# An SBUF allocator that rounds every buffer to 128 bytes in place of 64, in a two-layer mixer plus sparse-attention kernel on one core

## The chip, the cores and the metric

The kernel runs on one NeuronCore of one Trainium2 chip. The metric is the device time of one launch, in microseconds (us). All times below are of the hardware: either of plain runs, or of one execution that the hardware profiler recorded.

## The reference

The input is `x`, 512 tokens of 1024 channels, all in fp32. Two layers of a hybrid block come first, then one layer of sparse attention (NSA):

```python
for l in range(2):                       # first_block
    h = rmsnorm(x, norm_mix_g[l])
    proj = h @ w_in[l]                   # 1024 -> mLSTM q, k, v, o and gates, attention q, k, v, two branch gates
    hm = mlstm(...)                      # 4 heads, chunkwise
    ha = sliding_window_attention(...)   # 16 query heads, 4 key heads, window 128
    y = sigmoid(ga) * (hm @ w_branch_m[l]) + sigmoid(gb) * (ha @ w_branch_a[l])
    x = x + y @ w_out[l]
    h = rmsnorm(x, norm_mlp_g[l])
    x = x + square(relu(h @ w_up[l])) @ w_down[l]      # 1024 -> 4096 -> 1024
x = rmsnorm(x, final_norm_g)
u = rmsnorm(x, pre_norm_gain_2[0])       # second_block, one layer
out = x + rmsnorm(nsa_mixer(u, ...), post_norm_gain_2[0])
```

## The kernel before

Every activation is kept transposed: channels on the 128 partitions, the 512 tokens along the free axis, so that a 1024 x 512 activation is eight tiles `[128, 512]` of 2048 bytes per partition.

**Units.** Every weight matrix is cut into units of 1024 inputs by 128 outputs. One unit makes one `[128, 512]` output tile in PSUM. The 332 units of 512 KB come from `w_all` through one queue (SyncE, L426) into `w_raw`, two buffers in turn. Products are made in three parts so that fp32 precision is nearly kept with the faster fp32r type: ScalarE writes `w_hi` (the weights rounded to fp32r, L861), GpSimd writes `w_lo` (the rest, L446), and each activation likewise has a `hi` and a `lo` buffer. For each of the eight input tiles `quarter()` issues three matmuls of 512 columns: `w_hi` by `hi` (L485), `w_hi` by `lo` (L486) and `w_lo` by `hi` (L487). A unit is thus 24 matmuls, in four quarters of six. The stationary operand of each is a 128 x 128 block of `w_hi` or `w_lo` (512 bytes per partition), which TensorE loads (LDWEIGHTS, shown as PEld) while the matmul before still streams its 2048 bytes.

**Which buffer streams in which product.** The steps of the prediction need this list:

| buffers that stream | product | units of 24 matmuls in the whole kernel |
|---|---|---|
| `hT_hi/lo` | everything in the attention loops (`LOOP`, `NLOOP`), NSA's keys and values, the MLP's `up` | 200 |
| `hm_hi/lo` (the same bytes as `hT`) | `hm @ w_branch_m` (`MIX`) | 16 |
| `ha_hi/lo` | `ha @ w_branch_a` (`MIX`) | 16 |
| `y_hi/lo` | `y @ w_out`, two layers and NSA | 24 |
| `u_hi/lo` | the MLP's `down` | 64 |
| `hx_hi/lo` | the first products of each layer, before the norm is known | 12 |

`MIX` takes units of `hm` and `ha` in turn. The MLP runs four times per layer eight units of `up` and then eight of `down`. Two gate products of 24 matmuls (`gate_gemm`, L512 to L514) stream `hx` against weights of their own, `gw_hi/lo`, and a third streams `hT` against `gwn_hi/lo`. In the attention loops the quarters of the `hT` units are placed among short matmuls and transposes (the transposes have `ident` as the moving operand).

**The order of work** is written out by hand as lists of steps (`LOOP`, `MIX`, `MLP`, `NLOOP`, ...), and each engine walks the same lists; semaphores tie them together. Nothing in them depends on addresses.

**The allocator.** `new()` gives every buffer its byte offset within the partition. Without `at=` it takes the next free place, counted in `top`; with `at=a` it takes the next place of a list `a`, so that the same region can be laid out several times for different stages. The size is rounded up to 64 bytes before it is added. The first buffer starts at byte 16512, which is 129 times 128. The large buffers have sizes that are multiples of 512, so the offset of one buffer carries on to all behind it. The small ones do not: `vn` (96 bytes), `vcur` (80), `late` (4), then `vbuf` and `numsb` (4128 each), `gcur` (32).

Of the kernel before, what the change touches and what calls it, by code (L numbers as in the profile page):

```python
# [222 lines left out]
def two_layers_and_nsa(nc, w_all, wg_all, vec_it, vec_l, vec_n, ident_in, tri_in, onehot_w, onehot_n,  # L223
                       tab_w, tab_n, late_in, x_in, w1_in, w2_in, pos_in, scr_w, scr_n, out):
    ctx = ExitStack()
    with ctx:
# [5 lines left out]
        top = [base]  # L232

        def new(name, shape, dt=F32, at=None):
            size = -(-4 * int(np.prod(shape[1:])) // 64) * 64
            off = top[0] if at is None else at[0]
            t = nc.alloc_sbuf_tensor_at(name, shape, dt, offset=off)
            if at is None:
                top[0] += size
            else:  # L240
                at[0] += size
            return t

        x = new("x", [P, KT, S])
        hT_at = top[0]
        hT = [new("hT_hi", [P, KT, S], F32R), new("hT_lo", [P, KT, S], F32R)]
        raw = new("w_raw", [P, 2, KT * P])
        w_hi = new("w_hi", [P, 4, HALF], F32R)
        w_lo = new("w_lo", [P, 4, HALF], F32R)
# [1673 lines left out]
```

How the kernel before makes its waits and increments, by code:

```python
        @block.sync  # L410
        def _(sp):
            nc.sync.dma_start(vl[:, 0:DEPTH, :], vec_l).then_inc(gains_in, 16)
            nc.sync.dma_start(x[:, 0, :], x_in[0:P, :]).then_inc(x_landed[0], 16)
            nc.sync.dma_start(raw[:, 0, :], w_all[0]).then_inc(raw_in[0], 16)
            for k in range(2, KT, 2):
                nc.sync.dma_start(x[:, k, :], x_in[k * P:(k + 1) * P, :]).then_inc(x_landed[k], 16)
            nc.sync.dma_start(raw[:, 1, :], w_all[1]).then_inc(raw_in[1], 16)
            for dst, src in ((ident[:, :], ident_in), (tri[:, :], tri_in), (vit[:, :, :], vec_it),
                             (vn[:, :], vec_n), (late[:, :], late_in)):
                nc.sync.dma_start(dst, src).then_inc(cst_in, 16)
            with sp.Fori(0, UNITS // 2 - 1) as i:
                for p in range(2):
                    sp.wait_ge(lo_done, i * 4 + 2 * p + 6)
                    nc.sync.dma_start(raw[:, p, :], w_all[2 * i + p + 2]).then_inc(raw_in[p], 16)
            for k in range(KT):
                if k % 2 == 0:
                    sp.wait_ge(x_done, KT + k // 2 + 1)
                else:
                    sp.wait_ge(x_pool, k // 2 + 1)
                nc.sync.dma_start(out[k * P:(k + 1) * P, :], x[:, k, :]).then_inc(out_s, 16)
            sp.wait_ge(out_s, 16 * KT)
# [56 lines left out]
            def norm_sum(count, total=None):  # L491
                use = step_uses(w, ("norm_",))[0]
                pe.wait_ge(o_free[1], use.m + 1)
                pe.wait_ge(sq_used, count)
```

## Time and profile before

| | |
|---|---|
| median of 3 runs | 2405.76 us |
| lowest and highest | 2405.76 and 2406.56 us |
| the profiled execution's own time | 2405.57 us |
| its span, first to last instruction | 2403.5 us |
| mean granted TensorE clock | 0.982 |
| busy: TensorE matmul, weight load | 96%, 80% |
| busy: VectorE, ScalarE, GpSimd | 38%, 40%, 37% |
| DMA | 193.84 MB, 81 GB/s on average |

The chain of waits is the work that ended last, followed back from the end. In the timeline each row is one instruction; on TensorE the ends of matmuls are modelled, so that two neighbouring rows overlap in time, and what one matmul costs in a dense stretch is the distance between two starts.

### The profile page before, as it was taken

To read this page: it belongs to the slowest core of one execution; us is meant where nothing else is said; L and a number is where in the kernel's file an instruction comes from. 1 tells how busy PE (TensorE), PEld (TensorE's weight loads), DVE (VectorE), ACT (ScalarE), POOL (GpSimd) and SP (SyncE) were. 2 spreads that over 40 slices of the span, in tenths; PEclk is the share of its full clock that TensorE was granted. 3 is DMA by queue.
4 is the path that set the end of the run, shared out by engine and by line. 5 is a ranking of instruction groups with operands and counts; after the bars stand their busy time and mean duration, and the time that the engine had idled before them with its cause. 6 is when DMAs were issued, how large, how long until landed. Compare 5 with 4: busy or idle time off the path is not lost.

```text
span 2403.5 us, 35769 instructions
## 1 busy us (share of the span) xinstructions
PE 2317.2 (96%) x11397; PEld 1917.0 (80%) x11397; DVE 920.9 (38%) x1907; ACT 972.0 (40%) x2051; POOL 885.2 (37%) x672
## 2 busy tenths in 40 slices
PE   6999999999999998999999999999999999999996
PEld 4888888788888886888888788888887878888885
DVE  7343343324132136243343324132136335445452
ACT  4455455434232234455455434222234244445443
POOL 3333333444444444333333444444444321221213
PEclk9999999999999999999999999999999999999998
DMA  3221222222222222221222222222223221110202
GB/s 121 70 77 63 87 70 70 79 87 96 97 97 96 96 91 93 70 79 61 87 71 69 79 89 94 97 97 96 96 89 117 104 71 53 44 64 32 70 35 70
DMA packets 58793, 193.84 MB, mean 81 GB/s; under 512 B 6654, under 2 KB 11311, under 8 KB 58352
## 3 DMA queue, kind: packets, MB, share of 16 engines
q1 hardware_dynamic: 50400, 177.48, 21.7%
q10 hardware_dynamic: 8336, 15.60, 1.9%
q8 instruction: 36, 0.59, 0.1%
q14 instruction: 21, 0.17, 0.0%
HBM read 190.89 MB, written 2.16 MB: 80 GB/s over the span
## 4 chain that ended last, share of the span: by engine, by line
PE 89%; DVE 5%; ACT 2%; issue 2%; ACTq 0%; DVEq 0%; POOL 0%; POOLq 0%
PE ps L485 25%; PE ps L487 24%; PE ps L486 24%; PE ps L547 4%; PE ps L527 3%; PE ps L535 2%; PE ps L645 1%; PE ps L501 1%; PE ps L633 1%; PE ps L786 1%; PE ps L748 1%; PE ps L811 1%; DVE sz L1363 0%; DVE tn L1805 0%; ACT e_buf L908 0%
## 5 line engine op out<-in xcount | busy, mean ns | idle before, releaser
L446 POOL TENSOR_TENSOR w_lo<-w_raw,w_hi 128x512 fp32r<-128x512 f32 x664 | 878.6, 1327 | 1497.4 <-ACT w_hi L861 1493.5
L485 PE MATMUL ps<-hT_hi,w_hi 128*128 128x512 f32 x1600 | 653.6, 409 | 0.6 <-DVE qn L1333 0.6
L487 PE MATMUL ps<-hT_hi,w_lo 128*128 128x512 f32 x1600 | 630.9, 394 | 0.0
L486 PE MATMUL ps<-hT_lo,w_hi 128*128 128x512 f32 x1600 | 630.2, 394 | 0.0
L861 ACT ACTIVATE w_hi<-w_raw 128x512 fp32r<-128x512 f32 x664 | 411.3, 626 | 483.3 <-PE ps L487 455.3
L487 PEld LDWEIGHTS ps<-hT_hi,w_lo 128*128 128x128 f32 x1600 | 304.0, 190 | 66.8
L485 PEld LDWEIGHTS ps<-hT_hi,w_hi 128*128 128x128 f32 x1600 | 305.0, 191 | 64.4 <-issue 8.6
L486 PEld LDWEIGHTS ps<-hT_lo,w_hi 128*128 128x128 f32 x1600 | 305.1, 191 | 56.3 <-issue 0.5
L485 PE MATMUL ps<-u_hi,w_hi 128*128 128x512 f32 x512 | 201.7, 394 | 0.0
L486 PE MATMUL ps<-u_lo,w_hi 128*128 128x512 f32 x512 | 201.7, 394 | 0.0
L487 PE MATMUL ps<-u_hi,w_lo 128*128 128x512 f32 x512 | 201.7, 394 | 0.0
L1397 DVE TENSOR_TENSOR x<-x,ps 128x512 f32<-128x512 f32 x64 | 44.1, 688 | 267.4 <-PE ps L487 267.4
L1370 DVE SCALAR_TENSOR_TENSOR e_buf<-ps,rs 128x512 f32<-128x512 f32 x64 | 44.3, 692 | 213.2 <-PE ps L487 213.2
L487 PEld LDWEIGHTS ps<-u_hi,w_lo 128*128 128x128 f32 x512 | 95.7, 187 | 23.8
L485 PEld LDWEIGHTS ps<-u_hi,w_hi 128*128 128x128 f32 x512 | 95.8, 187 | 23.7
L486 PEld LDWEIGHTS ps<-u_lo,w_hi 128*128 128x128 f32 x512 | 95.8, 187 | 23.6
L912 ACT ACTIVATE u_hi<-e_buf 128x512 fp32r<-128x512 f32 x64 | 40.6, 634 | 175.0 <-DVE e_buf L1370 175.0
L991 ACT ACTIVATE Pn<-Ln,st 128x128 f32<-128x128 f32 (+3 forms) x128 | 71.7, 560 | 91.1 <-DVE st L1471 89.8
L991 ACT ACTIVATE Pb<-L,st 128x256 f32<-128x256 f32 (+1 forms) x128 | 61.4, 480 | 73.7 <-DVE st L1471 72.6
L1471 DVE CUSTOM_DVE_ANT_0 Ln<-ps,biasn 128x128 f32<-128x128 f32 (+3 forms) x128 | 62.1, 490 | 51.2 <-DVEq L1278 48.8
L1333 DVE SCALAR_TENSOR_TENSOR aq<-ps,aq 64x512 fp32r<-64x512 f32 x32 | 22.0, 689 | 154.3 <-ACT aq L886 153.7
L485 PE MATMUL ps<-y_hi,w_hi 128*128 128x512 f32 x192 | 75.9, 395 | 1.9 <-DVE y_lo L1813 1.9
(289 smaller groups left out, 3326.0 us busy)
## 6 DMA issues: line engine op xcount, KB each, us to landing
w_raw<-w_all SPq DMA_DIRECT2D x332, 512.0 KB, 3.2
bias<-scr_w ACTq DMA_DIRECT2D x8, 512.0 KB, 3.8
biasn<-scr_n ACTq DMA_DIRECT2D x4, 1024.0 KB, 5.2
w1k<-w_in ACTq DMA_DIRECT2D x2, 1024.0 KB, 8.4
w1v<-w_in ACTq DMA_DIRECT2D x1, 2048.0 KB, 15.0
out<-x SPq DMA_DIRECT2D x8, 256.0 KB, 2.0
x<-x_in SPq DMA_DIRECT2D x4, 256.0 KB, 6.3
x<-x_in ACTq DMA_DIRECT2D x4, 256.0 KB, 5.7
```

The costliest lines, as they stand in the source:

```text
L446: nc.gpsimd.tensor_tensor(w_lo[:, h, :], raw[:, h // 2, (h % 2) * HALF:(h % 2 + 1) * HALF], w_hi[:, h, :].bitcast(F32), ALU.subtract).then ...
L485: nc.tensor.matmul(ps[:, p, :], wh, hi[:, kk, :], start=(kk == 0), stop=False)
L486: nc.tensor.matmul(ps[:, p, :], wh, lo[:, kk, :], start=False, stop=False)
L487: last = nc.tensor.matmul(ps[:, p, :], wl, hi[:, kk, :], start=False, stop=(kk == KT - 1))
L527: last = nc.tensor.matmul(ps[:, 2 + us[0].b, 0:nk * P], q[:, hd, qt * P:(qt + 1) * P], kk[i][:, k0 * P:(qt + 1) * P], start=(i == 0), stop ...
L535: last = nc.tensor.transpose(ps[:, 4 + us[0].b, c * P:(c + 1) * P], pb[:, j % 3, c * P:(c + 1) * P], ident[:, :])
L547: last = nc.tensor.matmul(ps[:, 6 + ob, (qt % 2) * 256 + hd * DH:(qt % 2) * 256 + (hd + 1) * DH], pt[:, j % 3, c * P:(c + 1) * P], vv[:, k ...
L861: nc.scalar.activation(w_hi[:, 2 * p + h, :], raw[:, p, h * HALF:(h + 1) * HALF], ACT.Copy)\
L991: nc.scalar.activation(Pbuf[:, j % 3, 0:n], Lbuf[:, j % 2, 0:n], ACT.Exp, scale=-1.0, bias=st[:, 0, j:j + 1], accum_out=st[:, 1, j:j + 1]) ...
L1370: V.scalar_tensor_tensor(e_buf[:, e.b, :], g, 0.0, rs[:, :], ALU.max, ALU.mult).then_inc(g_free[u.b], 1)
L1397: V.tensor_tensor(x[:, n, :], x[:, n, :], g, ALU.add).then_inc(g_free[u.b], 1)
L1471: V.tensor_tensor_reduce(out=Lbuf[:, j % 2, 0:n], in0=ps[:, 2 + b_, 0:n], in1=reverse(bias_t, j % GH, n), scale=1.0, scalar=first, op0=ALU ...
```

## The change

One number in `new()`:

```diff
         def new(name, shape, dt=F32, at=None):
-            size = -(-4 * int(np.prod(shape[1:])) // 64) * 64
+            size = -(-4 * int(np.prod(shape[1:])) // 128) * 128
             off = top[0] if at is None else at[0]
```

What it does to the offsets follows from the code alone. The buffers from `x` to `late` stay where they are. `late` holds 4 bytes and now takes 128 in place of 64, so everything behind it moves by 64 bytes. In the attention loop's layout `vbuf` and `numsb` add 64 bytes each, so what follows them moves by 192. The offset within 512 bytes, of the buffers that the prediction names:

```
buffer                      before: offset, mod 512     after: offset, mod 512
hT_hi (hm_hi)                32896   128                 32896   128
w_hi, w_lo                   73856   128  82048  128     the same
ident                        90240   128                 the same
u_hi (u_lo 16384 behind)     97856    64                 97920   128
gw_hi                       101952    64                102016   128
y_hi, hx_hi                 130624    64                130688   128
ha_hi                       163392    64                163456   128
mqk                         163392    64                163456   128
Pb (behind vbuf, numsb)     208576   192                208768   384
gwn_hi                      220736    64                220800   128
```

Both layouts end below the limit that the code asserts, 229368 (before 228928, after 228992), and no two buffers overlap after that did not before.

## Rows read from the trace of the kernel before

**Rows 1.** The page: span, TensorE's busy time, and the chain's shares by engine.

```profile
span 2403.5 us, 35769 instructions
...
PE 2317.2 (96%) x11397; PEld 1917.0 (80%) x11397; DVE 920.9 (38%) x1907; ACT 972.0 (40%) x2051; POOL 885.2 (37%) x672
...
PE 89%; DVE 5%; ACT 2%; issue 2%; ACTq 0%; DVEq 0%; POOL 0%; POOLq 0%
```

**Rows 2.** Busy us (count) by stretch: PE, PEld, DVE, ACT, POOL; granted clock; DMA.

```profile
575.00:607.00 32.00, 32.00 (x142) 26.47 (x141) 14.03 (x18) 11.64 (x20) 17.53 (x13) 1.00 0.26 91
615.00:657.00 42.00, 42.00 (x182) 33.66 (x181) 5.52 (x8) 9.93 (x16) 20.14 (x16) 1.00 0.29 95
```

**Rows 3.** Timeline, TensorE, mixing products: start us, us, engine, line, operation.

```profile
441.08 0.39 PE L485 MATMUL ps<-ha_hi,w_hi 128*128 128x512 f32 x1
...
446.68 0.39 PE L485 MATMUL ps<-hm_hi,w_hi 128*128 128x512 f32 x1
...
448.06 0.39 PE L485 MATMUL ps<-hm_hi,w_hi 128*128 128x512 f32 x1
...
452.14 0.39 PE L485 MATMUL ps<-ha_hi,w_hi 128*128 128x512 f32 x1
```

**Rows 4.** Timeline, TensorE, from the `w_out` product to the second `up`.

```profile
524.10 0.39 PE L485 MATMUL ps<-y_hi,w_hi 128*128 128x512 f32 x1
...
568.90 0.39 PE L485 MATMUL ps<-hT_hi,w_hi 128*128 128x512 f32 x1
...
613.35 0.39 PE L485 MATMUL ps<-u_hi,w_hi 128*128 128x512 f32 x1
...
658.15 0.39 PE L485 MATMUL ps<-hT_hi,w_hi 128*128 128x512 f32 x1
...
701.69 0.39 PE L485 MATMUL ps<-u_hi,w_hi 128*128 128x512 f32 x1
```

**Rows 5.** Timeline, TensorE, layer 0: the gate product, then a V unit.

```profile
33.15 0.39 PE L512 MATMUL ps<-hx_hi,gw_hi 128*128 128x512 f32 x1
...
35.19 0.40 PE L485 MATMUL ps<-hx_hi,w_hi 128*128 128x512 f32 x1
...
37.06 0.40 PE L487 MATMUL ps<-hx_hi,w_lo 128*128 128x512 f32 x1
```

**Rows 6.** Timeline, TensorE, the last layer's gate product.

```profile
1856.59 0.39 PE L512 MATMUL ps<-hT_hi,gwn_hi 128*128 128x512 f32 x1
...
1859.34 0.39 PE L512 MATMUL ps<-hT_hi,gwn_hi 128*128 128x512 f32 x1
```

**Rows 7.** Groups by form, TensorE: mean ns of one after the comma.

```profile
L486 PE MATMUL ps<-u_lo,w_hi 128*128 128x512 f32 x512 | 201.7, 394 | 0.0
...
L486 PE MATMUL ps<-y_lo,w_hi 128*128 128x512 f32 x192 | 75.7, 395 | 0.0
...
L486 PE MATMUL ps<-ha_lo,w_hi 128*128 128x512 f32 x128 | 50.4, 394 | 0.0
...
L486 PE MATMUL ps<-hx_lo,w_hi 128*128 128x512 f32 x96 | 39.5, 411 | 0.0
```

**Rows 8.** Timeline, TensorE: `hT` quarters among the mLSTM products.

```profile
113.02 0.40 PE L486 MATMUL ps<-hT_lo,w_hi 128*128 128x512 f32 x1
...
115.33 0.39 PE L487 MATMUL ps<-hT_hi,w_lo 128*128 128x512 f32 x1
```

**Rows 9.** Groups by form, TensorE: short matmuls.

```profile
L535 PE MATMUL ps<-ident,Pb 128*128 128x128 f32 x224 | 46.9, 279 | 5.0 <-DVE hm L1627 4.6
...
L633 PE MATMUL ps<-mqk 128*128 128x128 f32 x160 | 23.0, 274 | 0.0
```

**Rows 10.** Groups by form, VectorE.

```profile
L1397 DVE TENSOR_TENSOR x<-x,ps 128x512 f32<-128x512 f32 x64 | 44.1, 688 | 267.4 <-PE ps L487 267.4
...
L1387 DVE TENSOR_TENSOR y_lo<-t,y_hi 128x512 f32 x16 | 11.1, 693 | 14.1 <-ACT y_hi L915 14.1
```

**Rows 11.** Timeline, GpSimd, one unit's weight halves in an `up` product.

```profile
599.18 2.77 POOL L446 TENSOR_TENSOR w_lo<-w_raw,w_hi 128x512 fp32r<-128x512 f32 x2 [2.67 <-ACT w_hi L861]
```

## The prediction

> **What bounds the kernel now.** The page first: TensorE is busy for 2317.2 of a span of 2403.5 us, and the chain of waits is 89% TensorE, 5% VectorE, 2% ScalarE [rows 1]. Then the busy time by stretch: inside an `up` product and inside a `down` product TensorE is busy without a break (32.00 of 32 us, 42.00 of 42) at granted clock 1.00, the 2.4 GHz level, while the other three engines have idle time [rows 2]. So only what changes the pace of matmuls, or a wait of TensorE, can move the end. The change adds and removes no instruction, moves no step, no DMA and no semaphore. It moves addresses alone, and so the question is whether any pace in the trace goes with addresses.
>
> For that I read the timeline of TensorE and measured the distance between starts. The mixing products are the cleanest place, since units of `hm` and `ha` take turns there, with the same weight buffers, the same PSUM banks and the same engines beside them. The unit of `ha` takes 446.68 - 441.08 = 5.60 us, that of `hm` 452.14 - 446.68 = 5.46 us [rows 3]. The last 18 matmuls of the `hm` unit take 4.08 us, which is **226.7 ns** each; the 24 of `ha` take **233.3 ns** each. The first six of `hm`, behind `ha`, take 1.38 us (230 ns each): the pace needs a few matmuls to settle, which costs about 0.02 us an entry.
>
> The same two paces stand in the long products, of 8 units or 192 matmuls [rows 4]. The second `up`, which streams `hT`: 701.69 - 658.15 = 43.54 us, 226.8 ns each. `down`, which streams `u`: 658.15 - 613.35 = 44.80 us, 233.3 ns. `w_out`, which streams `y`: 568.90 - 524.10 = 44.80 us, 233.3 ns.
>
> **What goes with it.** Take the distance of the streaming buffer from the weight buffer, by the offset table of the change. `hT` and `hm` stand at 128 in 512, the weights `w_hi` and `w_lo` too: they are congruent, and fast. `u`, `y`, `ha` stand at 64: slow. The trace has a test that keeps the streaming buffer and changes only the weights. In layer 0 the gate product streams `hx` (64) against `gw` (64 in 512, congruent): nine starts in 35.19 - 33.15 = 2.04 us, 226.7 ns. The next unit streams the same `hx` against `w` (128): eight starts in 37.06 - 35.19 = 1.87 us, 233.8 ns [rows 5]. And the last layer's gate product streams the fast buffer `hT` (128) against `gwn` (64): 12 starts in 1859.34 - 1856.59 = 2.75 us, 229.2 ns, between the two [rows 6]. Neither the buffer alone, nor its region, nor the bank explains all five; whether stationary and streaming operand are congruent does. Within `hT` units the distance takes many multiples of 512 (weights step by 512 bytes, tiles by 2048) and the pace holds, so congruent in 512 is enough. After the change `u`, `y`, `hx`, `ha`, `gw` and `gwn` all stand at 128 in 512, as `w` does.
>
> **The sum.** Each entry is matmuls by 233.3 - 226.7 = 6.6 ns. The counts are three times those of the groups [rows 7].
> - `u`: 64 units in 8 products. Each is worth 44.80 - 43.54 = 1.26 us [rows 4], so 10.1 us.
> - `y`: 24 units, three products of the same size, 3.8 us.
> - `ha`: 16 units of 24 matmuls, 384 by 6.6 ns = 2.5 us, and 16 entries of `hm` behind `ha` that are no longer unsettled, 16 by 0.02 = 0.3 us [rows 3].
> - `hx`: 288 matmuls. Their mean is 411 where the settled ones have 394 [rows 7], since some run at the lower clock level or behind a wait; I count 240, by 6.6 ns = 1.6 us, less 0.1 for entries.
> - `up` behind `y` or `u`: 8 entries by 0.02 = 0.2 us. The gate product on `gwn`: 24 by 2.5 ns, 0.1 us.
>
> Together 10.1 + 3.8 + 2.8 + 1.5 + 0.3 = **18.5 us**. All but `hx` lies where TensorE never waits, so it reaches the end whole.
>
> **Is there cover to lose?** A faster `down` asks for a unit of weights every 5.44 us in place of 5.60. `up` does so already: there GpSimd, the last in the supply, takes 2.77 us for the two halves of a unit and then waits 2.67 us for ScalarE [rows 11], and DMA is busy 0.26 [rows 2]. `down` has less beside it on VectorE and ScalarE than `up` has. So no new wait.
>
> **What may move besides.** (1) `hT` quarters among the short matmuls of the attention loops run unsettled: 10 starts in 2.31 us, 231 ns [rows 8]. These are 12 units by 8 iterations plus 8 by 4, 128 units or 3072 matmuls, in 512 quarters. Their own buffers don't move, but the short matmuls before them do. If they came out settled, the gain is at most 512 entries by 0.02 = 10 us; many quarters follow each other directly, so I estimate 6.5. If they settled later or never, the loss is at most 3072 by 6.6 = 20 us less what is paid now. I take nothing. (2) The short matmuls. `mqk` against itself, congruent, has a mean of 274; `ident` against `Pb`, 64 apart in 128, has 279 [rows 9]; some 860 transposes change from apart to congruent in 128, so 860 by 5 ns bounds it at 4 us either way. I take nothing, since idle time and settling are in these means too. (3) VectorE and ScalarE. `x` at 0 in 128 has 688 ns, `y_lo` with all operands at 64 has 693 [rows 10]. With 5% of the span on VectorE's part of the chain, some 170 such operations, that is at most 1 us. I take nothing.
>
> The profiled execution of before took 2405.57 us, 2.1 us around its span, and stands 0.2 us under the median of the runs, 2405.76. The forecast is 2405.57 - 18.5 = 2387.1 for such an execution, **2387.3 us** against the median.
>
> **The rivals.** *Nothing changes, 2405.8 us, chance 0.10.* The two paces would belong to something else that differs between these products, such as which engine wrote the streaming buffer last. For it: VectorE and ScalarE do different work beside `down`, and the price is only 16 cycles of 2.4 GHz per matmul. Against it: rows 3 and rows 5, where the pace flips from one matmul to the next. A rule speaks for this rival. The Trainium skill's page "SBUF — State Buffer" (the section "A bandwidth-pool intuition that's wrong") gives TensorE a second, independent read port for the weight load, and its specifications know only cachelines of 16 bytes; both 64 and 128 are multiples of these, and with independent ports the distance of the two operands could not matter. By that rule the sum is 0.
>
> *Slower, 2419 us, chance 0.03.* The place is the attention loops. Their short matmuls change their distance to the `hT` stream, and its settling is lost: 3072 matmuls at 233.3 instead of what I take as 226.7 plus 6.5 us in all, 20 - 6.5 = 13.5 us more. Alone it gives 2405.8 + 13.5 = 2419; it decides only if the 18.5 us fail too, or shrink below the loss. For it: `hT` there is unsettled behind short matmuls now. Against it: these short matmuls were partly congruent with one another before, and `hT` settles behind them.
>
> *More than the sum, down to 2380.8 us, chance 0.15.* The quarters among short matmuls settle at once, 6.5 us on top.
>
> **How the numbers follow.** The forecast has 0.72, the case above it 0.15, no change 0.10, slower 0.03. The first two are faster by far more than 0.2%, 4.8 us, which is about what a measurement of this kernel can tell from no change; so faster has 0.87, within it 0.10, slower 0.03. The range reaches down to 2380 for the settled quarters, and up to 2393: 4 us for the transposes and 1.5 us for an `hx` gain that waits hide. It leaves out the other two cases, 0.13, and a forecast mis-sized by more than these bounds.
>
> **What would show it.** In the changed kernel every `down` and `w_out` product of eight units takes 43.5 us, and the units of `ha` and `hm` take the same 5.44 us. `hx` against `w` runs at 226.7 ns a start. The `up` products stay at 43.5. The counts of instructions are the same. Wrong would be: `down` still at 44.8 (the first rival), or `down` at 43.5 with a span that doesn't follow, which would put a loss in the attention loops.

## The result, and the profile after

The changed kernel takes **2388.18 us** (median of 6 runs, 2387.30 to 2392.55), the kernel before 2405.81 (6 runs, 2405.35 to 2406.80). The ratio is 0.9929, with a 95% interval of 0.9916 to 0.9942: 17.6 us less. The forecast was 2387.3, the range 2380 to 2393. The profiled execution took 2387.97 us.

The page of the kernel after, the lines that answer to [rows 1]:

```profile
span 2385.8 us, 35769 instructions
...
PE 2298.5 (96%) x11397; PEld 1918.5 (80%) x11397; DVE 921.1 (39%) x1907; ACT 971.7 (41%) x2051; POOL 885.2 (37%) x672
...
PE 89%; DVE 5%; ACT 2%; issue 2%; ACTq 0%; DVEq 0%; POOL 0%; POOLq 0%
```

The shares of the chain are the same, and so are the counts. TensorE's busy time fell by 18.7 us, the span by 17.7 us. So the time went out of the matmuls themselves and not out of waits.

The timeline of TensorE in the mixing products, as [rows 3]:

```profile
441.73 0.39 PE L485 MATMUL ps<-ha_hi,w_hi 128*128 128x512 f32 x1
...
447.17 0.39 PE L485 MATMUL ps<-hm_hi,w_hi 128*128 128x512 f32 x1
...
452.61 0.39 PE L485 MATMUL ps<-ha_hi,w_hi 128*128 128x512 f32 x1
```

Both kinds of unit take 447.17 - 441.73 = 5.44 and 452.61 - 447.17 = 5.44 us. Before they took 5.60 (`ha`) and 5.46 (`hm`). The unit of `hm` has also lost its 0.02 us of settling.

The long products, as [rows 4]:

```profile
523.33 0.39 PE L485 MATMUL ps<-y_hi,w_hi 128*128 128x512 f32 x1
...
566.85 0.39 PE L485 MATMUL ps<-hT_hi,w_hi 128*128 128x512 f32 x1
...
611.28 0.39 PE L485 MATMUL ps<-u_hi,w_hi 128*128 128x512 f32 x1
...
654.80 0.39 PE L485 MATMUL ps<-hT_hi,w_hi 128*128 128x512 f32 x1
...
698.32 0.39 PE L485 MATMUL ps<-u_hi,w_hi 128*128 128x512 f32 x1
```

`w_out` (the stream `y`), `up` (`hT`), `down` (`u`) and `up` again take 43.52, 44.43, 43.52 and 43.52 us. The first `up` holds the norm's matmul and was 44.45 before. A product of eight units on `y` or `u` has gone from 44.80 to 43.52 us, 192 matmuls at 226.7 ns.

`hx` against `w` in layer 0, as the second and third of [rows 5], and then the gate product on `gwn`, as [rows 6]:

```profile
35.55 0.39 PE L485 MATMUL ps<-hx_hi,w_hi 128*128 128x512 f32 x1
...
37.36 0.39 PE L487 MATMUL ps<-hx_hi,w_lo 128*128 128x512 f32 x1
```

```profile
1840.31 0.39 PE L512 MATMUL ps<-hT_hi,gwn_hi 128*128 128x512 f32 x1
...
1843.03 0.39 PE L512 MATMUL ps<-hT_hi,gwn_hi 128*128 128x512 f32 x1
```

Eight starts in 1.81 us, 226 ns (before 233.8), and twelve in 2.72 us, 226.7 ns (before 229.2).

Mean durations of forms, as [rows 7, 9, 10], and one unit's weight halves on GpSimd, as [rows 11]:

```profile
L486 PE MATMUL ps<-u_lo,w_hi 128*128 128x512 f32 x512 | 199.2, 389 | 0.0
...
L486 PE MATMUL ps<-ha_lo,w_hi 128*128 128x512 f32 x128 | 49.8, 389 | 0.0
...
L535 PE MATMUL ps<-ident,Pb 128*128 128x128 f32 x224 | 46.9, 279 | 5.0 <-DVE hm L1627 4.7
...
L633 PE MATMUL ps<-mqk 128*128 128x128 f32 x160 | 23.0, 274 | 0.0
...
L1397 DVE TENSOR_TENSOR x<-x,ps 128x512 f32<-128x512 f32 x64 | 44.0, 688 | 257.2 <-PE ps L487 257.2
...
L1387 DVE TENSOR_TENSOR y_lo<-t,y_hi 128x512 f32 x16 | 11.1, 693 | 14.1 <-ACT y_hi L915 14.1
```

```profile
591.67 2.77 POOL L446 TENSOR_TENSOR w_lo<-w_raw,w_hi 128x512 fp32r<-128x512 f32 x2 [2.67 <-ACT w_hi L861]
```

The modelled duration of a matmul on `u` or `ha` went from 394 to 389 ns. The two short matmuls have 279 and 274 ns as before, the two VectorE operations 688 and 693 as before, and GpSimd still works 2.77 us and then waits 2.67.

**Where the 17.7 us of span are.** From the starts of each stage, before minus after: eight `down` products, 10.2 us; the two layers' `w_out`, 2.6; the 32 mixing units, 2.8; the eight `up`, 0.2; the gate product on `gwn`, 0.1. That is 15.9 us. The third `w_out`, NSA's, has the same pace, 1.3 us less, but took 0.5 us longer as a whole. The other 1.8 us are thus a balance of larger pieces, and these are mostly stretches of TensorE at its lower clock level (1.2 in place of 2.4 GHz). Here are the first units of `hm` in layer 1, and NSA's output product on `y` (columns: busy us and count of PE, PEld, DVE, ACT, POOL; granted clock; DMA). Before:

```profile
1332.00:1344.00 12.00, 9.13 (x34) 7.38 (x34) 10.30 (x18) 10.75 (x21) 2.85 (x2) 0.86 0.12 44
2338.00:2386.00 48.00, 44.70 (x191) 35.39 (x189) 9.53 (x15) 16.96 (x31) 16.88 (x13) 1.00 0.17 55
```

After:

```profile
1325.00:1337.00 12.00, 9.13 (x42) 7.40 (x41) 10.10 (x18) 11.39 (x23) 2.55 (x2) 1.00 0.12 44
2320.00:2368.00 48.00, 44.90 (x190) 36.20 (x188) 9.16 (x14) 16.72 (x30) 16.66 (x13) 0.96 0.17 55
```

In the first row the clock was 0.86 before and is 1.00 after, which saved 1.6 us of layer 1's mixing. In the second it was 1.00 and is 0.96, which took back the 1.3 us of NSA's `w_out` and 0.5 more. Ahead of both stretches TensorE waits for VectorE, 2.9 us and 1.9 to 2.0, but it does so in both kernels, so the wait alone doesn't decide. In a repetition of the changed kernel (after_5, below) the stretch in layer 1's mixing was there and the one in layer 0's mixing was not, so such stretches come and go between executions of one kernel. The one in NSA's output product is there in all eight other traces of whole kernels, and the trace of before is the only one without it.

NSA's loops, from the end of the gate product to the output product, are 1.9 us shorter. Before 2337.41 - 1860.03 = 477.38 us, after 2319.15 - 1843.71 = 475.44:

```profile
1860.03 0.39 PE L485 MATMUL ps<-hT_hi,w_hi 128*128 128x512 f32 x1
...
2337.41 0.48 PE L485 MATMUL ps<-y_hi,w_hi 128*128 128x512 f32 x1
```

```profile
1843.71 0.39 PE L485 MATMUL ps<-hT_hi,w_hi 128*128 128x512 f32 x1
...
2319.15 0.47 PE L485 MATMUL ps<-y_hi,w_hi 128*128 128x512 f32 x1
```

Most of it is a clock stretch again. The same 120 matmuls of the last round of NSA's loop, before and after:

```profile
2242.10:2267.65 25.55, 24.14 (x121) 19.39 (x120) 10.32 (x18) 10.54 (x22) 7.97 (x6) 0.87 0.32 103
```

```profile
2225.52:2249.47 23.95, 22.56 (x122) 18.27 (x120) 10.21 (x18) 10.54 (x22) 7.92 (x6) 0.93 0.35 109
```

They take 1.6 us less at this one place, where the granted clock was 0.87 and is 0.93; only the other 0.3 us come in small steps. Four more executions with congruent layouts (below) have 475.4 to 475.5 us for the whole of the loops; in two of them (after_5, late_only) the step of 1.6 us stands one round earlier. The three with offsets apart have 477.3 (r32_64), 477.5 (pad128) and 479.6 (w64, where `hT` is slow too). So the layout seems to move this stretch, but how isn't shown. For the short matmuls, of which the prediction takes nothing, 0.3 us at most are left here.

The attention loops of the two layers became 0.3 and 0.7 us longer. In the four other executions with congruent layouts they vary between 0.7 us shorter and 0.6 longer, and that goes with how long the lower level lasts at their start: in the first 20 us of layer 1's loops the granted clock was 0.66 before and is 0.62 after, in layer 0's 0.65 and 0.64.

Taken together, the pace gave 15.9 + 1.3 = 17.2 us, the small steps in NSA 0.3, and the clock stretches gave 1.6 twice and took 1.8 (NSA's `w_out`) and 1.0 (the two layers' loops, if all of it is the clock's), 0.4 in sum.

### The profile page after: what moved, and what is told of

Read it like the earlier page. It is cut to its first block, busy times and chain, and to the rows that moved or that the text cites. A ratio compares the mean times of both kernels' runs of the same rounds, so it can differ in the third digit from the quotient of the medians.

```text
span 2385.8 us, 35769 instructions
## 1 busy us (share of the span) xinstructions
PE 2298.5 (96%) x11397; PEld 1918.5 (80%) x11397; DVE 921.1 (39%) x1907; ACT 971.7 (41%) x2051; POOL 885.2 (37%) x672
## 4 chain that ended last, share of the span: by engine, by line
PE 89%; DVE 5%; ACT 2%; issue 2%; ACTq 0%; DVEq 0%; POOL 0%; POOLq 0%
PE ps L485 25%; PE ps L487 24%; PE ps L486 24%; PE ps L547 4%; PE ps L527 3%; PE ps L535 2%; PE ps L645 1%; PE ps L501 1%; PE ps L633 1%; PE ps L786 1%; PE ps L748 1%; PE ps L811 1%; DVE sz L1363 0%; DVE tn L1805 0%; ACT e_buf L908 0%
```

## The experiments

The theory at the start: the pace of an fp32r matmul of 512 columns goes by the distance of its moving operand's start from that of its stationary operand, modulo 128 bytes. Its rivals: the absolute alignment of the operands, the moving operand's alone, and contention with the other engines.

### A map of distances with TensorE alone (map1)

The kernel computes nothing of the model. It makes buffers of zeros, runs 48 matmuls of 128x512 for each pair of offsets, and writes zeros. It was run once, like the other maps. Its core, in place of the whole program:

```diff
+for c, (a, b) in enumerate(COMBOS):
+    for k in range(48):
+        nc.tensor.matmul(ps[:, c % 7, :], wt[:, a + P * (k % 4):a + P * (k % 4) + P], mv[:, b:b + S],
+                         start=(k == 0), stop=(k == 47))
```

> Only TensorE works here: 48 matmuls of 128x512 fp32r for each of 27 pairs of offsets (stationary, moving), nothing of the model is computed and the output is zeros. My theory (the distance between stationary and moving operand, taken modulo 128 bytes, sets the pace): pairs with distance 0 in 128 run at 226.7 ns a start, (0,64), (0,192), (64,0), (64,128) at 233.3 or between, (64,64), (16,16), (32,32), (96,96) at 226.7. Rival 1 (the absolute start counts: 128-byte aligned operands are fast): (64,64), (16,16), (32,32) and (96,96) are slow, 233.3. Rival 2 (contention with the other engines that write and read beside the stream): all pairs run alike, at 226.7 or less, as nothing else runs. What 16, 32, 48 and 80 bytes give I do not know; between 226.7 and 233.3 if the settling is gradual.

Measured, as the mean distance between starts of the last 31 matmuls of each pair, in ns:

```
stationary, moving:  0,0     0,64    0,128   0,192   0,256   0,320   0,384   0,448
                     226.7   228.8   232.3   233.3   226.7   228.8   232.3   233.3
stationary, moving:  64,64   128,128 96,96   32,32   64,0    64,128  64,192  128,0   192,0
                     226.7   226.7   226.7   226.7   233.4   229.0   232.2   232.6   228.9
stationary, moving:  0,4     0,8     0,16    0,32    0,48    0,80    0,96    0,112   16,16
                     236.7   233.2   231.8   233.3   233.4   231.2   233.3   231.3   229.9
```

Busy time by stretch of the first run through distances 0, 128 and 192, and of (64,0):

```profile
15.00:25.00 10.00, 10.00 (x46) 8.29 (x45) 0.00 (x0) 0.00 (x0) 0.00 (x0) 1.00 0.00 0
37.00:47.00 10.00, 10.00 (x45) 8.10 (x44) 0.00 (x0) 0.00 (x0) 0.00 (x0) 1.00 0.00 0
48.00:58.00 10.00, 10.00 (x44) 8.03 (x43) 0.00 (x0) 0.00 (x0) 0.00 (x0) 1.00 0.01 2
204.00:214.00 10.00, 10.00 (x44) 8.01 (x44) 0.00 (x0) 0.00 (x0) 0.00 (x0) 1.00 0.01 2
```

In 10 us at the 2.4 GHz level 46 matmuls touch the stretch at distance 0, 44 at distance 192 or -64, and the other engines are at 0.00. So the pace needs no other engine: the contention rival fell. The absolute start fell too, for multiples of 32 bytes: (32,32), (64,64), (96,96) and (128,128) are as fast as (0,0). For other starts something absolute is left, since (16,16) has 229.9 at distance 0. And the theory itself is mended in two places. The period is **256 bytes and not 128**, and the distance has a sign: +64 gives 228.8, -64 gives 233.3. That explains the 229.2 of `gwn` in [rows 6], where the stream stands 64 above the weights, beside the 233.3 of `u`, which stands 64 below.

### Padding behind `late` alone (late_only, late_only_5)

```diff
         late = new("late", [P, 1])
+        top[0] += 64
         st = new("st", [P, 12, 16])
```
on the kernel before, with its rounding to 64.

> The rounding to 64 as before, with 64 bytes of padding behind late alone. Theory: all long products are congruent with their weights modulo 128, as in the changed kernel, so the whole gain stands: 2388, ratio 0.993. Rival (the buffers behind vbuf and numsb, in the attention loops, carry part of it): they are 64 apart from ident and from the weights of hT here, so some of the gain is missing, 2390 or more.

2390.24 us (4 runs), ratio 0.9936 (0.9919 to 0.9953). The long products were at 43.52, but the median lay 2 us above the changed kernel's, and so the two were timed again side by side.

> The changed kernel itself again, timed beside the next one on the same chip: 2388 us.

> The kernel before with 64 bytes of padding behind late, again, beside the changed kernel. Theory: the whole gain is the distance of the long products, which is the same in both; 0 to 1 us apart. Rival: rounding vbuf and numsb too is worth the 2 us by which the medians of the earlier runs differ (2390.2 and 2388.2).

2388.46 us for the changed kernel, 2388.74 for the padding alone (5 runs each), with ratios of 0.9928 (0.9914 to 0.9941) and 0.9931 (0.9918 to 0.9945). They are equal. Of all that the change of the rounding does, the 64 bytes behind `late` are what counts. The rest is worth nothing that can be measured: `vbuf` and `numsb`, and 64 bytes each behind `gat` (192 bytes, which moves `vgs`, `vgf` and `tn` of NSA by 128) and behind the small tables `tabw` and `tabn`, which the text on the change doesn't list.

### Everything moved by 64 (all64)

```diff
-        base = 16512
+        base = 16512 + 64
```
on the changed kernel.

> The changed kernel with every buffer moved up by 64 bytes (the base is 16576). Theory (distance): no pair changes its distance, 2388 us. Rival 1 (absolute alignment to 128): every fp32r product runs at 233.3 ns a start, which is 18.5 us of gain lost and up to 28 us more for hT and hm, about 2434 us.

2387.39 us (2 runs), ratio 0.992 (0.990 to 0.994). `down` and `up` in its timeline:

```profile
610.62 0.39 PE L485 MATMUL ps<-u_hi,w_hi 128*128 128x512 f32 x1
...
654.14 0.39 PE L485 MATMUL ps<-hT_hi,w_hi 128*128 128x512 f32 x1
...
697.66 0.39 PE L485 MATMUL ps<-u_hi,w_hi 128*128 128x512 f32 x1
```

43.52 us and 43.52 us, with every start at 64 in 128. Being aligned to 128 is of no use in itself.

### The weights moved by 64 against everything (w64)

```diff
+        top[0] += 64
         w_hi = new("w_hi", [P, 4, HALF], F32R)
         w_lo = new("w_lo", [P, 4, HALF], F32R)
+        top[0] += 64
         ident = new("ident", [P, P])
```
on the changed kernel.

> The changed kernel with only w_hi and w_lo moved by 64 bytes against the buffers that stream (the buffers behind them move by 128). Theory (distance): all 332 units are 64 apart and run at 233.3 ns a start, u, y, ha, hx lose their 18.5 us, hT and hm lose 5184 by 6.66 ns less the 6.5 us that hT pays now for settling, 28 us; about 2434 us. Rival (only the moving operand's own start counts): moving operands are at multiples of 128, 2388 us.

2421.94 us (2 runs), ratio 1.0064 (1.0044 to 1.0084): slower than before, but 12 us short of the 2434 expected. `down` and the next `up`:

```profile
619.55 0.39 PE L487 MATMUL ps<-u_hi,w_hi 128*128 128x512 f32 x1
...
663.50 0.39 PE L487 MATMUL ps<-hT_hi,w_hi 128*128 128x512 f32 x1
...
708.29 0.39 PE L487 MATMUL ps<-u_hi,w_hi 128*128 128x512 f32 x1
```

`down` takes 43.95 us (228.9 ns) and `up` 44.79 (233.3 ns). `hT` stands 64 below the weights and is slow, as expected. `u` stands at 256 in 512 and the weights at 192, so it is 64 above them and pays a third only. That is the sign of the map, now in the model kernel. The moving operand's own start, at multiples of 128 for all, would have given 2388: that rival fell too. The weights' own start doesn't do it either, since all64 has them at the same 192 in 512 and is fast.

### 128 bytes more (pad128), and two distances at once (r32_64)

```diff
         late = new("late", [P, 1])
+        top[0] += 128
         st = new("st", [P, 12, 16])
```
on the changed kernel: all starts are still multiples of 128.

> The changed kernel with 128 more bytes behind late: every buffer still starts at a multiple of 128, but u, y, ha, hx stand 128 from their weights modulo 256. Theory (modulo 256): 232.3 ns a start for these, 2784 by 5.6 = 15.6 us slower than the changed kernel, about 2403.8 us; a product of eight units takes 44.6 us. Rival (modulo 128, as predicted before the result): 2388 us, 43.5 us.

2406.30 us (10 runs), ratio 1.000 (0.999 to 1.0009): **the whole gain is gone**. Its timeline from `w_out` to the second `up`:

```profile
523.64 0.40 PE L486 MATMUL ps<-y_hi,w_hi 128*128 128x512 f32 x1
...
568.45 0.39 PE L486 MATMUL ps<-hT_hi,w_hi 128*128 128x512 f32 x1
...
612.88 0.40 PE L486 MATMUL ps<-u_hi,w_hi 128*128 128x512 f32 x1
...
657.67 0.39 PE L486 MATMUL ps<-hT_hi,w_hi 128*128 128x512 f32 x1
...
701.21 0.40 PE L486 MATMUL ps<-u_hi,w_hi 128*128 128x512 f32 x1
```

`w_out` takes 44.81 us, `down` 44.79 (233.3 ns) and `up` after it 43.54. In the model kernel distance 128 costs the full 6.6 ns, not the 5.6 of the map, which is 2784 by 1.0 = 2.8 us, about the 2.5 us by which the total came out above the expectation. The period of 256 holds, that of 128 fell.

```diff
+        top[0] += 64
         r32_at = top[0]
         top[0] += 32768
+        top[0] += 64
         sig_at = top[0]
```
on the changed kernel: `u` at +64, `y`, `ha`, `hx` at +128.

> The changed kernel with u (and what else lies in its region) at +64 from the weights, and y, ha, hx at +128. Theory (modulo 256): down takes 43.9 us for eight units (228.8 ns), w_out 44.6 (232.3 ns); total 1536 by 2.1 + 1248 by 5.6 = 10.2 us above the changed kernel, 2398.4 us. Rival (modulo 128): w_out stays at 43.5 us, down goes to 44.8; the total is the same, the stages tell them apart.

2400.56 us (8 runs), ratio 0.9975 (0.9964 to 0.9985). `w_out`, `up`, `down`:

```profile
524.53 0.40 PE L487 MATMUL ps<-y_hi,w_hi 128*128 128x512 f32 x1
...
569.33 0.39 PE L487 MATMUL ps<-hT_hi,w_hi 128*128 128x512 f32 x1
...
613.76 0.40 PE L487 MATMUL ps<-u_hi,w_hi 128*128 128x512 f32 x1
...
657.72 0.40 PE L487 MATMUL ps<-hT_hi,w_hi 128*128 128x512 f32 x1
```

`w_out` 44.80 and `down` 43.96 us. The two distances have their own price in one kernel, each where the map puts it; only +128 is again 233.3 and not 232.3. The total is 2.2 us above the expectation; this dearer +128 is 1248 by 1.0 = 1.2 us of it, and the rest wasn't followed up.

### Is there a still better layout? (map2)

The same probe with the model kernel's triple (`w_hi` by `hi`, `w_hi` by `lo`, `w_lo` by `hi`) and all 64 combinations of 0, 64, 128, 192 for `hi`, `lo` and `w_lo`:

```diff
+nc.tensor.matmul(ps[:, c % 7, :], wh_, mv[:, h + j:h + j + S], start=(k == 0), stop=False)
+nc.tensor.matmul(ps[:, c % 7, :], wh_, lo[:, l + j:l + j + S], start=False, stop=False)
+nc.tensor.matmul(ps[:, c % 7, :], wl_, mv[:, h + j:h + j + S], start=False, stop=(k == N // 3 - 1))
```

> Only TensorE works; the output is zeros. Per combination 16 times the model's triple (w_hi by hi, w_hi by lo, w_lo by hi), for all residues 0, 64, 128, 192 of hi, lo and w_lo against w_hi. Theory now (signed distance moving minus stationary, modulo 256, from the first map): all three at distance 0 run at 226.7 ns; hi and lo at +64 at 228.8, at +128 at 232.3, at +192 at 233.3, with w_lo at 0; mixed triples give a mean of their three distances' paces, so none is faster than 226.7. Rival (the distance that counts is that of the stream to the next block that is being loaded, not to its own): mixed triples are not that mean, and w_lo at another residue than w_hi slows one matmul in three although hi's distance to its own block is 0 in none of the neighbours. If any triple is under 226.0 ns there is a layout better than the changed kernel's.

All at 0: 226.65 ns, and again at the end of the run. The next best are 228.8 (`hi` at 128 with the rest at 0, for one), the worst 235.5 (192, 128, 128). With `w_lo` alone at 64, 128 or 192 the triple has 231.1 to 231.5, though two of its three matmuls have distance 0. So a triple is not the mean of its distances: one operand out of line costs between 2.2 (`hi` at 128, or `lo` at 192) and 7.9 ns (`hi` at 192) on average of the three. No combination of these beats the layout of the changed kernel.

### Own block or next block? (map4)

```diff
+a, b = (wa // 4, ma // 4) if k % 2 == 0 else (wb // 4, mb // 4)
```
Blocks and streams take turns, so that a stream's distance to its own block and to the one loaded meanwhile differ.

> Only TensorE works; the output is zeros. Two kinds of matmul take turns, so that the distance of a stream to its own block and to the next block (the one that is loaded while it runs) can be set apart. Theory N (the load of the next block meets the running stream): (0,128,128,0), whose own distances are 128 but whose next distances are 0, runs at 226.7 ns, and (0,128,0,128), whose own are 0 and next 128, at 232 to 233; likewise (0,64,64,0) fast and (0,64,0,64) slow. Theory O (the distance to its own block counts): the reverse.

Own 0, next 128: 228.3. Own 128, next 0: 230.0. Own 0, next 64: 231.7. Own 64, next 0: 231.6. Own 0, next 192: 231.7. Own 192, next 0: 233.4 (in the pairs of 64 and 192 the sign changes from matmul to matmul). Only all alike has 226.7. **Inconclusive**: neither theory holds, both distances seem to count, and what meets in the memory stays open. The run showed one thing more: streams at +64 had 233.35 here, where map1 had 228.8 for the same pair. The starts repeat in another pattern of steps. The two runs differ in what ran before and in the PSUM bank (map2 had 228.9 at +64 in the same bank, so the bank alone isn't it); that the order of work decides is likely, but not tested.

### Width and type (map3)

```diff
+nc.tensor.matmul(ps[:, c % 7, 0:n], w_[:, a + P * (k % 4):a + P * (k % 4) + P], m_[:, b:b + n],
```

> Only TensorE works; the output is zeros. Width and type. Theory: an fp32r stream of 256 or 384 columns pays up to the same 6.6 ns a matmul where its own duration and not the weight load sets the pace; at 256 columns the weight load may hide it. Distances 512 and 1024 are 0 modulo 256: 226.7. (24,24) and (48,48), which are not multiples of 32, are slower than 226.7 although their distance is 0, as (16,16) was with 229.9. bf16 has half the bytes per column: if the cost is one of bytes fetched per stream, less than 6.6 ns or nothing; if it is one of the two reads meeting in the same bank, the same 6.6 ns.

ns a start, by distance:

```
                     0       32      64      128     192
fp32r, 512 columns   226.7   233.3   228.8   232.3   233.3   (32 to 192 from map1)
fp32r, 384 columns   173.3           173.3   175.9   174.6
fp32r, 256 columns   120.0           117.8   118.7   113.3
bf16, 512 columns    215.8   215.8   215.8   215.8   215.8
bf16, 256 columns    109.2   109.2   109.2   109.2   109.2
```

Distances of 512 and 1024 gave 226.7, as expected. (24,24) had 233.3 and (48,48) 231.1: not multiples of 32, and slow at distance 0. bf16 shows no effect at any of these distances. And at 256 columns of fp32r distance 0 is the slowest and 192 the fastest.

## Why the prediction was right, point by point

**The bound.** The prediction held that only the pace of matmuls could move the end. TensorE's busy time fell by 18.7 us, the span by 17.7.

**What goes with the pace.** The step rested on the five pairs of the trace, and each of them moved as said. The statement that congruent in 512 is enough is right; the experiments showed that 256 is what it takes. My expectations for the first experiments were narrower than the prediction's own ground: they said 128, and w64 came out 12 us below for it. [rows 6] had the sign in it (229.2 at +64 against 233.3 at -64), and I read it only as "between the two".

**The sum.** The terms of `u` and `y` were 1.26 us a product and measured 1.28; `ha` and `hm` came out as written, 5.44 and 5.44; `up` 0.02 an entry. The term of **`hx`, 1.5 us, was mis-sized: it measured nothing**, the stages on `hx` together being 0.1 us longer than before. The pace came as forecast: over the `hx` matmuls that follow one another at the 2.4 GHz level it saved 1.4 us. But these stages end in waits of TensorE for VectorE and ScalarE, and there the time came back. Two of them, from the list of TensorE's waits before (us in total, times, longest):

```profile
PE ps L501 <- DVE vtmp L1311: 4.8, 1, 4.8
...
PE ps L485 <- DVE x2k L1323: 3.7, 1, 3.7
```

and after:

```profile
PE ps L501 <- DVE vtmp L1311: 5.2, 1, 5.2
...
PE ps L485 <- DVE x2k L1323: 4.0, 1, 4.0
```

The two others, in layer 0, went from 7.1 to 7.4 (L1500) and from 2.7 to 2.9 us (L961). In the first of the rows VectorE works without a break on the gates before it comes to `vtmp`, from 947.2 to 956.0 us of the trace of before and from 939.8 to 948.6 after, so VectorE and not the pace of the matmuls sets the end of the stage. The prediction had named this for the upper end of its range only, "waits that hide it".

The other terms promised 17.0 us and gave 17.2. The clock stretches were not in the prediction at all. They gave and took pieces of 1 to 2 us, and that they left only 0.4 us in sum is luck; the rest of the agreement is not.

**Cover.** None was lost: in `up` GpSimd works 2.77 us and waits 2.67 of each 5.44, as before, and `down` keeps that pace.

**What might have moved besides.** The unsettled quarters did not settle: where `hT` matmuls follow one another in layer 0's loops their starts are 228.6 ns apart on average before and 228.7 after, and the two layers' attention loops are within 0.7 us of before. The short matmuls read 279 and 274 ns as before, the VectorE operations 688 and 693. VectorE's busy time went from 920.9 to 921.1 us.

**The rivals.** *Nothing changes* fell with the first stage. With it fell the reading of the Trainium skill's page "SBUF — State Buffer" (the section "A bandwidth-pool intuition that's wrong (but worth ruling out)", and its specifications) that two independent read ports and cachelines of 16 bytes leave no room for it: map1 shows 226.7 and 233.3 ns with nothing but TensorE at work and both starts multiples of 64. *Slower* did not come, as the `hT` streams keep settling behind short matmuls (228.7 ns, above). *More than the sum* did not either.

## What to carry to other kernels

Where fp32r matmuls of 512 columns fill TensorE, put the starts of the stationary and the moving buffers on the same remainder modulo 256 bytes and at multiples of 32, and look for two paces of the same matmul in the timeline to find out whether they are. Rounding sizes to 128 is not that rule: it worked here because the parity came out right, and one more buffer of up to 128 bytes between the weights and these streams takes the 17.6 us away again, as 128 bytes of padding did. Such a change is worth up to 3% of the time of the matmuls that it touches (226.7 in place of 233.3 ns), nothing for bf16, and at 256 columns it may cost. What meets in the memory or in the engine to make the difference is open.

## What the runs showed that I had not expected

- The period of 256 bytes and the sign: 228.8 ns at +64, 233.3 at -64, at a floor of 226.7.
- bf16 streams of 512 columns run at 215.8 ns whatever the distance, 10.9 ns less than the best fp32r.
- At 256 columns of fp32r distance 0 has 120.0 ns and distance 192 has 113.3.
- Two repeating patterns for one pair of offsets, 228.8 and 233.35 ns; what chooses between them is open.
- Stretches at the lower clock level of 1.5 to 2 us of cost each come and go between layouts and executions, and hide or mimic a gain of 0.1% here.
